# Computing the u and p projections of a hybrid decoder step with features on the partitions

## The chip, the cores and the metric

The kernel runs on one core of a Trainium2 chip, in float32. The metric is the device time of one execution in microseconds (us). The core's engines are TensorE (PE; its weight loads are the row PEld), VectorE (DVE), ScalarE (ACT), GpSimd (POOL) and SyncE (SP), which issues most DMAs. Every engine works through its own queue in order, and they wait for one another on semaphores.

## The reference

One inference step of one layer, over 1024 prompt tokens and 64 new tokens (8 sequences of 8), width 1024:

```
h = rmsnorm(x, norm1_g);  proj = h @ w_in                       # 1024 -> 3 x 512
uv = gelu(proj[..., :1024]);  u = uv[..., :512]
v = layernorm(uv[..., 512:], a_norm_g, a_norm_b);  p = proj[..., 1024:]
ya = u * (tril(W_s[h]) @ v_chunk + b[h])                        # 4 heads, chunks of 128 positions
yb = ((trailing mean of p over 2/4/8/16) - p) @ b_w[g] * b_scale    # 4 groups of 128 features
x = x + concat(ya, yb) @ w_out
h2 = rmsnorm(x, norm2_g)
x = x + top-1 of 4 groups, then top-2 of 8 SwiGLU experts (h2);  y = rmsnorm(x, normf_g)
# also returned: the last 15 rows of p of the prompt and of each new sequence, and v of the new tokens
```

## The kernel before

**Front.** The tokens are nine tiles: tiles 0 to 7 of 128 prompt tokens, tile 8 ("sample") of 64. `pipeline` (L342) writes every engine's queue as steps: step i has the projections and mixers of tile i (`cur`), the residual, second norm and router of tile i-1 (`prev`), the ranking of tile i-2 (`pprev`) and the first norm and turn of tile i+1 (`nxt`). Steps 2 to 6 are a hardware loop, the others straight code.

In a step TensorE makes for `cur` the products v, u, p (L1182: hT, features on partitions and tokens as columns, is the stationary operand; w_in streams in 512 columns; eight contraction slices of 128). ScalarE takes gelu of v and u and a copy of p. VectorE normalises v (L929 to L944). TensorE forms z = W_s v for the four heads (L1193), with tokens on partitions. It forms the pooled means by products with constant band matrices (L1205), one for the tile itself and one for the tile before, whose p VectorE keeps in `ptail` (L957); these products leave features on the partitions. VectorE gates z with bias and u into `ya` (L953). TensorE turns xn of tile i+1 into the PSUM banks 0 and 1 (`wide`, L1131), turns `ya` (L1131), and multiplies the pooled means by b_w (L1221). VectorE reads the turned xn into hT (L822) and scales yb (L964). TensorE turns xn2 of tile i-1 into the same banks 0 and 1, which is why it waits for hT_ready; then it multiplies by the first half of w_out (L1239), makes the router's logits (L1247) and the second half of w_out (L1255). Tile 8 does its products in two halves of the array (L1144, L1153), 64 tokens each.

**Expert part.** 32 experts in blocks of 96, 80 or 64 rows. For each block w1 and w3 are the stationary operand, 64 features at a time into one half of the array, and the tokens are the columns (L1285, contraction slice outer, group of 128 features inner); the down product is L1306. Each expert's 6 MB of weights come in six chunks into a ring of 18 (three experts). SyncE issues a load when the chunk in its place is used (L472), for the first experts in places of w_in and x that the front has left: L456 after the sample's projections, L475 to L484 after the first rows are gathered and the last out_b. GpSimd writes the token table (L553), gathers and scatters rows. ScalarE reads the table's first column (L733) once the table of tiles 0 to 7 is written; this releases the first gather.

## Time and profile before

| | us |
|---|---|
| median of 3 runs (lowest, highest) | 977.61 (976.02, 978.34) |
| the profiled execution | 981.23 |
| its span | 979.6 |
| TensorE busy in the span | 900.6 |
| VectorE, ScalarE, GpSimd busy | 257.5, 110.0, 155.4 |

Rows of the profile read as: busy time, instructions, mean ns of one, and what ended an idle time ("<-"). A float32 matmul shows as two instructions. Start times are us from the start of the span. PEclk is the granted TensorE clock as a share of full speed. The front ends at about 397 us, the expert part at about 943 us.

### The profile page before, as it was taken

Reading aid. Unit: us, or ns where it says so; the run is one execution under the profiler, and the core shown is the slowest. Engines: PE = TensorE matmul, PEld = TensorE weight load, DVE = VectorE, ACT = ScalarE, POOL = GpSimd, SP = SyncE. Lnnn points to the kernel's source line nnn. Section 1 sums busy time; section 2 is a strip of 40 time slices with the busy share of each in tenths; the row PEclk is TensorE's granted clock in tenths of the full one; section 3 lists DMA queues with packets and bytes.
Section 4 is the critical chain, followed back from the end, with each engine's and each line's share of the span. In section 5 each row is a group of like instructions: output and inputs, shape, how many; then the busy total and the mean of one; then the engine's idle time right before and its main releaser. Section 6 shows DMA issues by size and latency. Waiting matters only on the chain.

```text
span 979.6 us, 24674 instructions
## 1 busy us (share of the span) xinstructions
PE 900.6 (92%) x10538; PEld 596.2 (61%) x10538; DVE 257.5 (26%) x779; ACT 110.0 (11%) x173; POOL 155.4 (16%) x260
## 2 busy tenths in 40 slices
PE   4999999999999995799999999999999999989940
PEld 2545555454554563767868686868686768567630
DVE  1443454625445356150010101010101010100106
ACT  0210111101111011101001000001010101001013
POOL 1000100000000000211213131312122313113110
PEclk9999999999999997699999999999999999979985
DMA  8870200201021027799999999999999999999738
GB/s 340 275 292 1 87 31 12 86 0 43 8 78 44 3 91 286 301 399 392 353 393 404 393 407 391 408 389 409 389 408 391 402 394 401 398 405 400 270 70 321
DMA packets 57440, 258.70 MB, mean 264 GB/s; under 512 B 10809, under 2 KB 11889, under 8 KB 40356
## 3 DMA queue, kind: packets, MB, share of 16 engines
q1 hardware_dynamic: 47484, 238.51, 60.7%
q0 software_dynamic: 9264, 19.36, 8.1%
q8 instruction: 41, 0.67, 0.3%
q10 hardware_dynamic: 640, 0.07, 0.1%
q14 instruction: 11, 0.09, 0.0%
HBM read 240.86 MB, written 25.04 MB: 271 GB/s over the span
## 4 chain that ended last, share of the span: by engine, by line
PE 54%; issue 3%; DVE 2%; DMA 2%; DVEq 0%; ACT 0%; SPq 0%; POOLq 0%; POOL 0%
PE ps L1285 31%; PE ps L1306 19%; PE ps L1131 3%; DVE big L1115 1%; DMA big<-x_rows 1%; DMA x_rows<-xn,sidx 0%; PE ps L1319 0%; DMA xg<-h_rows,oidx 0%; PE ps L1314 0%; DVE ssf L806 0%; DVE ssf L805 0%; DVE ssf L808 0%; DVEq L80 0%; ACT junk L784 0%; DMA slot_table<-ids,dest 0%
## 5 line engine op out<-in xcount | busy, mean ns | idle before, releaser
L1285 PEld LDWEIGHTS ps<-hT,big 128*64 128x64 f32 x8192 | 299.5, 139 | 41.1 <-issue 39.1
L1285 PE MATMUL ps<-hT,big 128*64 128x80 f32 (+2 forms) x8192 | 308.6, 236 | 13.0 <-issue 10.7
L1306 PE MATMUL ps<-big,poolT 128*80 128x512 f32 (+2 forms) x512 | 191.2, 594 | 0.6 <-issue 0.6
L1182 PE MATMUL ps<-big,hT 128*128 128x512 f32 x384 | 168.9, 599 | 4.3 <-DMA big<-in_w_in 2.9
L1182 PEld LDWEIGHTS ps<-big,hT 128*128 128x128 f32 x384 | 72.8, 192 | 95.0 <-issue 88.0
L1306 PEld LDWEIGHTS ps<-big,poolT 128*80 128x80 f32 (+2 forms) x512 | 64.5, 149 | 103.1 <-issue 102.0
L1079 DVE TENSOR_TENSOR poolT<-u,ps 128x320 f32<-128x320 f32 (+2 forms) x32 | 15.5, 486 | 421.7 <-PE ps L1285 421.7
L577 POOL DMA_INDIRECT x_rows<-xn,sidx x22 | 32.9, 1495 | 274.1 <-ACT xn L763 253.1
L553 POOL DMA_INDIRECT slot_table<-ids,dest x18 | 18.9, 1052 | 305.4 <-DVE dest L879 263.3
L1239 PE MATMUL ps<-big 128*128 128x512 f32 x128 | 56.4, 593 | 0.9 <-DVE big L964 0.9
L1255 PE MATMUL ps<-big 128*128 128x512 f32 x128 | 57.0, 598 | 0.0
L763 ACT ACTIVATE xn<-ps,gslot 80x1024 f32<-80x1024 f32 (+1 forms) x21 | 23.3, 1110 | 259.1 <-PE ps L1306 259.1
L1239 PEld LDWEIGHTS ps<-big 128*128 128x128 f32 x128 | 23.7, 190 | 28.0 <-issue 27.8
L1255 PEld LDWEIGHTS ps<-big 128*128 128x128 f32 x128 | 23.7, 190 | 27.6 <-issue 27.3
L572 POOL DMA_INDIRECT gslot<-gate_rows,pidx x32 | 32.2, 1007 | 21.3 <-POOL sidx L623 14.0
L996 DVE TENSOR_TENSOR hT<-ps,g2t 128x768 f32<-128x768 f32 (+1 forms) x32 | 28.0, 875 | 27.6 <-PE ps L1131 18.3
L1131 PE MATMUL ps<-ident,xn 128*128 128x128 f32 (+1 forms) x144 | 21.3, 297 | 13.2 <-DVE xn L817 8.4
L577 POOL DMA_INDIRECT x_rows<-bands,sidx x10 | 14.6, 1460 | 89.2 <-DVE bands L1086 76.0
L754 ACT ACTIVATE u<-ps 128x320 f32<-128x320 f32 (+2 forms) x32 | 13.9, 435 | 125.2 <-PE ps L1285 125.2
L1131 PEld LDWEIGHTS ps<-ident,xn 128*128 128x128 f32 (+1 forms) x144 | 18.6, 196 | 14.5 <-issue 9.6
L953 DVE SCALAR_TENSOR_TENSOR big<-ps,bst,u 128x128 f32<-128x128 f32 x32 | 9.0, 345 | 67.6 <-PE ps L1193 67.6
L695 ACT ACTIVATE xn<-big 128x1024 f32 (+2 forms) x9 | 9.5, 1057 | 150.3 <-DVE big L911 150.3
(184 smaller groups left out, 561.2 us busy)
## 6 DMA issues: line engine op xcount, KB each, us to landing
big<-in_exp_w SPq DMA_DIRECT2D x192, 1024.0 KB
big<-in_w_in SPq DMA_DIRECT2D x4, 1536.0 KB, 13.4
big<-in_w_out SPq DMA_DIRECT2D x2, 2048.0 KB, 14.4
x_rows<-big SPq DMA_DIRECT2D x8, 512.0 KB
h_rows<-xn SPq DMA_DIRECT2D x8, 512.0 KB, 2.9
big<-x_rows SPq DMA_DIRECT2D x8, 512.0 KB, 7.2
out_y_prompt<-big SPq DMA_DIRECT2D x8, 512.0 KB, 2.8
big<-in_x_prompt SPq DMA_DIRECT2D x1, 3072.0 KB, 11.3
```

The costliest lines, as they stand in the source:

```text
L553: pool.indirect_dma_start(slot_table, bass.IndirectOffsetOnAxis(ap=dest[0:m, j, c:c + 1], axis=0), ids[0:m, j, c, :], None, bounds_check=N ...
L572: pool.indirect_dma_start(dst, None, gate_rows, bass.IndirectOffsetOnAxis(ap=idx.bitcast(U32), axis=0), bounds_check=last_pair, oob_is_err ...
L577: pool.indirect_dma_start(x3_rows, bass.IndirectOffsetOnAxis(ap=idx.bitcast(U32), axis=0), src, None, bounds_check=last_row, oob_is_err=Tr ...
L763: act.activation(ys[s][0:m, :], ps[0:m, 5:7, :].rearrange("p a n -> p (a n)"), ACT.Copy, scale=gslot[s][0:m, 0:1]).then_inc(y_ready, 1)
L996: dve.tensor_tensor(xT[:, :, 0:ways * i].rearrange("p k (w i) -> p k w i", i=i), wide.rearrange("p k (i w) -> p k w i", w=WAYS)[:, :, 0:wa ...
L1079: dve.tensor_tensor(hhT[:, :, 0:m], s1T[:, :, 0:m], up3[:, :, 0:m], ALU.mult).then_inc(hhT_ready, 1)
L1131: last = pe.transpose(ps[:, bank + c // 4, (c % 4) * P:(c % 4) * P + m], xs[:, c, :], ident[0:m, 0:m])
L1182: last = pe.matmul(ps[0:m, bank, :], hT[:, k, 0:m], win[:, k, part * AW:(part + 1) * AW], start=(k == 0), stop=(k == KD - 1))
L1239: last = pe.matmul(ps[0:m, 6, :], yT[:, k, 0:m], wout[:, k, 0:512], start=(k == 0), stop=(k == KD - 1))
L1255: last = pe.matmul(ps[0:m, 7, :], yT[:, k, 0:m], wout[:, k, 512:D], start=(k == 0), stop=(k == KD - 1))
L1285: last = pe.matmul(out[c * w:(c + 1) * w, j, 0:m], up_weights(n)[:, k, j * P + c * w:j * P + (c + 1) * w], xT[:, 4 * half + k, 0:m], start ...
L1306: last = pe.matmul(ps[first:first + m, 5 + cols, :], hhT[:, 2 * half + k, 0:m], down_weights(n)[:, k, cols * 512:(cols + 1) * 512], start= ...
```

## The change

In tiles 0 to 7 u and p are computed with features on the partitions and tokens as columns: w_in is the stationary operand, 64 features at a time into alternate halves of the array, and hT streams in 128 columns. The contraction slices are the outer and the groups of 128 features the inner loop. v stays as it was; the order is v, p, u. z is computed turned as well, by exchanging the operands. So `ya` and the pooled means are born in the form that the output product needs: the turns of `ya` and the band products are gone. The trailing sums are made by VectorE along the columns (`pool_tile`), with 16 columns carried over from the tile before (`pT[:, :, 0:HALO]`), and the bias, now along the columns, comes from a tile broadcast to all partitions. ScalarE copies p into pT and no longer copies the pooled means and the turned ya. The bias and the share numbers live in `gf`, so the final gain is loaded into it late, in tile 8. The last rows of p of the prompt are turned back by four small products in tile 7 and stored from `xg[1]`. Tile 8 is computed as before.

```diff
-        vg, p, ya, ptail = [big[:, third + (NT + 1) * D + i * AW:third + (NT + 1) * D + (i + 1) * AW] for i in range(4)]
+        vg, ya, p, _ = [big[:, third + (NT + 1) * D + i * AW:third + (NT + 1) * D + (i + 1) * AW] for i in range(4)]
...
-        band = bands[:, 0:AW].rearrange("p (g n) -> p g n", n=P)
-        band_prev = bands[:, AW:D].rearrange("p (g n) -> p g n", n=P)
+        pT = bands[:, 0:GROUPS * (HALO + P)].rearrange("p (g n) -> p g n", n=HALO + P)
+        sum4 = bands[:, GROUPS * (HALO + P):GROUPS * (HALO + P) + 3 * (HALO + P)].rearrange("p (g n) -> p g n", n=HALO + P)
+        tail = third + (NT + 1) * D + 2 * AW
+        sum2 = big[:, tail:tail + GROUPS * (HALO + P)].rearrange("p (g n) -> p g n", n=HALO + P)
...
+        bias = gf[:, 0:AW].rearrange("p (h n) -> p h n", n=P)
+        share = gf[:, AW:AW + GROUPS * HALO].rearrange("p (g n) -> p g n", n=HALO)
...
-            load(bst[:, :], bs_th)
-            load(band_first[:, :, :], c_band_first)
+            load(bias_in[:, :], bs_th.rearrange("t h -> (t h)").partition_broadcast(P))
...
-            load_late(gf[:, :], normf_g.partition_broadcast(P))
...
             sp.wait_ge(v_ready, NT)
+            sp.wait_ge(yaT_ready, LAST)
+            sp.dma_start(gf[:, :], normf_g.partition_broadcast(P)).then_inc(in_gf, 16)
             sp.dma_start(v_s[0].rearrange("b s c -> (b s) c"), v[0:NS, :]).then_inc(outs, 16)
             sp.wait_ge(proj_p, NT)
+            sp.wait_ge(proj_u, NT)
             for n in range(CH):
                 sp.dma_start(chunk_dst(n, n), chunk_src(FIRST, n)).then_inc(chunk_in[n], 16)
...
+            pool.wait_ge(outs, 16 * OUTS)
...
-                    act.wait_ge(proj_u, i + 1)
-                    reached(act, ya_ready, i)
-                    take(u, 3, cur, ACT.Gelu).then_inc(u_gelu, 1)
-                    act.wait_ge(proj_p, i + 1)
-                    reached(act, ptail_ready, i)
+                    if cur != "sample":
+                        act.wait_ge(proj_p, i + 1)
+                        reached(act, halo_ready, i + 1)
+                        act.activation(pT[:, :, HALO:], ps[:, 4, :].rearrange("p (g n) -> p g n", n=P), ACT.Copy)\
+                            .then_inc(p_copied, 1)
+                        act.wait_ge(proj_u, i + 1)
+                        reached(act, yaT_ready, i)
+                        take(u, 3, cur, ACT.Gelu).then_inc(u_gelu, 1)
+                    if isinstance(i, int) and i == LAST - 1:
+                        act.wait_ge(trash_zeroed, 16)
+                        act.wait_ge(rows_turned, 1)
+                        act.activation(xg[1][0:HALO, 0:AW], ps[0:HALO, 4, :], ACT.Copy).then_inc(rows_copied, 1)
                     if cur == "sample":
...
                 reached(dve, proj_p, i)
+                reached(dve, proj_u, i)
...
+            def pool_tile(i, first):
+
+                at = lambda t, lo, by=0, gs=slice(0, GROUPS): t[:, gs, lo - by:HALO + P - by]
+                dve.wait_ge(p_copied, i + 1)
+                reached(dve, yb_done, i)
+                dve.tensor_tensor(at(sum2, 2), at(pT, 2), at(pT, 2, 1), ALU.add).then_inc(sum_step, 1)
+                dve.wait_ge(sum_step, 4 * i + 1)
+                dve.tensor_tensor(at(sum4, 4, 0, slice(0, 3)), at(sum2, 4, 0, slice(1, 4)), at(sum2, 4, 2, slice(1, 4)), ALU.add)\
+                    .then_inc(sum_step, 1)
+                dve.wait_ge(sum_step, 4 * i + 2)
+                dve.tensor_tensor(at(sum2, 8, 0, slice(2, 4)), at(sum4, 8, 0, slice(1, 3)), at(sum4, 8, 4, slice(1, 3)), ALU.add)\
+                    .then_inc(sum_step, 1)
+                dve.wait_ge(sum_step, 4 * i + 3)
+                dve.tensor_tensor(sum4[:, 2, HALO:], sum2[:, 3, HALO:], sum2[:, 3, HALO - 8:HALO - 8 + P], ALU.add)\
+                    .then_inc(sum_step, 1)
+                dve.wait_ge(sum_step, 4 * i + 4)
+                sums = (sum2[:, 0, :], sum4[:, 0, :], sum2[:, 2, :], sum4[:, 2, :])
+                for g, w in enumerate(WINDOWS):
+                    last = dve.scalar_tensor_tensor(poolT[:, g, :], sums[g][:, HALO:], 1.0 / w, pT[:, g, HALO:],
+                                                    ALU.mult, ALU.subtract)
+                if first:
+                    last.then_inc(share_step, 1)
+                    dve.wait_ge(share_step, 8)
+                    for g in range(GROUPS):
+                        last = dve.tensor_tensor(poolT[:, g, 0:HALO], sums[g][:, HALO:2 * HALO], share[:, g, :], ALU.mult)
+                    last.then_inc(share_step, 1)
+                    dve.wait_ge(share_step, 9)
+                    last = dve.tensor_tensor(poolT[:, :, 0:HALO], poolT[:, :, 0:HALO], pT[:, :, HALO:2 * HALO], ALU.subtract)
+                last.then_inc(poolT_ready, 1)
+                dve.tensor_copy(pT[:, :, 0:HALO], pT[:, :, P:HALO + P]).then_inc(halo_ready, 1)
+
...
+                if isinstance(i, int) and i == 0:
+                    dve.wait_ge(in_small, 16 * len(small))
+                    dve.tensor_copy(bias[:, :, :], bias_in.rearrange("p (t h) -> p h t", h=HEADS)).then_inc(share_step, 1)
+                    dve.wait_ge(share_step, 7)
+                if cur and cur != "sample":
+                    pool_tile(i, cur == "first")
+                    dve.wait_ge(z_done, i + 1)
+                    dve.tensor_tensor(ya[:, :], ps[:, 5, :], bias.rearrange("p h n -> p (h n)"), ALU.add).then_inc(z_biased, 1)
+                    dve.wait_ge(z_biased, i + 1)
+                    dve.wait_ge(u_gelu, i + 1)
+                    reached(dve, out_b, i)
+                    dve.tensor_tensor(yT[:, 0:HEADS, :], ya.rearrange("p (h n) -> p h n", n=P),
+                                      u.rearrange("p (h n) -> p h n", n=P), ALU.mult).then_inc(yaT_ready, 1)
+                if cur == "sample":
...
-                    for bank, part, free, done in () if cur == "sample" else \
-                            ((2, 1, v_gelu, proj_v), (3, 0, u_gelu, proj_u), (4, 2, p_copied, proj_p)):
-                        reached(pe, free, i)
-                        if bank == 2:
-                            reached(pe, logits_ready, i - 1)
+                    else:
+                        reached(pe, v_gelu, i)
+                        reached(pe, logits_ready, i - 1)
                         for k in range(KD):
-                            if isinstance(i, int) and i == 0 and bank == 2 and k % 2 == 0:
+                            if isinstance(i, int) and i == 0 and k % 2 == 0:
                                 pe.wait_ge(in_win[k // 2], 16)
-                            last = pe.matmul(ps[0:m, bank, :], hT[:, k, 0:m], win[:, k, part * AW:(part + 1) * AW],
+                            last = pe.matmul(ps[:, 2, :], hT[:, k, :], win[:, k, AW:2 * AW],
                                              start=(k == 0), stop=(k == KD - 1))
-                        last.then_inc(done, 1)
+                        last.then_inc(proj_v, 1)
+                        for bank, part, free, done in ((4, 2, p_copied, proj_p), (3, 0, u_gelu, proj_u)):
+                            reached(pe, free, i)
+                            for k in range(KD):
+                                for j in range(AW // P):
+                                    for c in range(SPLIT):
+                                        at = part * AW + j * P + c * NS
+                                        last = pe.matmul(ps[c * NS:(c + 1) * NS, bank, j * P:(j + 1) * P],
+                                                         win[:, k, at:at + NS], hT[:, k, :], start=(k + j == 0),
+                                                         stop=(k == KD - 1), skip_group_check=True)
+                            last.then_inc(done, 1)
...
-                        last = pe.matmul(ps[0:m, 5, h * P:(h + 1) * P], w[0:m, h, 0:m],
-                                         v[0:m, h * P:(h + 1) * P], start=True, stop=True)
+                        if cur == "sample":
+                            last = pe.matmul(ps[0:m, 5, h * P:(h + 1) * P], w[0:m, h, 0:m],
+                                             v[0:m, h * P:(h + 1) * P], start=True, stop=True)
+                        else:
+                            last = pe.matmul(ps[:, 5, h * P:(h + 1) * P], v[:, h * P:(h + 1) * P], w[:, h, :],
+                                             start=True, stop=True)
                     last.then_inc(z_done, 1)
...
-                    parts = {"first": [(p, band_first, P)], "mid": [(p, band, P), (ptail, band_prev, P)],
-                             "sample": [(p, band_s, NS), (state, band_state, DEC * STATE)]}[cur]
-                    w = P // SPLIT if cur == "sample" else P
...
+                    if isinstance(i, int) and i == LAST - 1:
+                        pe.wait_ge(p_copied, i + 1)
+                        for g in range(GROUPS):
+                            last = pe.matmul(ps[0:HALO, 4, g * P:(g + 1) * P], pT[:, g, P:HALO + P], ident[:, :],
+                                             start=True, stop=True, skip_group_check=True)
+                        last.then_inc(rows_turned, 1)
...
-                    pe.wait_ge(ya_ready, i + 1)
-                    turn(ya, m, yaT_done, HEADS, 5)
+                    if cur == "sample":
+                        pe.wait_ge(ya_ready, 1)
+                        turn(ya, m, yaT_done, HEADS, 5, whole=True)
                     pe.wait_ge(poolT_ready, i + 1)
+                    reached(pe, x2a_ready, i)
```

TensorE in a middle step of the loop, from the projections to the first half of the output product. Names: ps is PSUM, big holds w_in, w_out, p, ya and yT, done_early the masked W_s and b_w, bands the band matrices. Before:

```order
L1182 MATMUL ps<-big,hT 128x512 [waits p_copied]
L1182 MATMUL ps<-big,hT 128x512 x7
L1193 MATMUL ps<-v,done_early 128x128 [waits rank_taken,v_ready]
L1193 MATMUL ps<-v,done_early 128x128 x3
L1205 MATMUL ps<-bands,big 128x128 [waits x2a_ready,ptail_ready,p_copied]
L1205 MATMUL ps<-bands,big 128x128 x7
...
L1131 MATMUL ps<-ident,xn 128x128 [waits h2T_ready,xn_ready]
L1131 MATMUL ps<-ident,xn 128x128 x7
L1131 MATMUL ps<-ident,big 128x128 [waits ya_ready]
L1131 MATMUL ps<-ident,big 128x128 x3
L1221 MATMUL ps<-poolT,done_early 128x128 [waits poolT_ready]
L1221 MATMUL ps<-poolT,done_early 128x128 x3
```

And in the change, to the turns of xn2 and the output product (L1326):

```order
L1258 MATMUL ps<-hT,big 64x128 [waits u_gelu]
L1258 MATMUL ps<-hT,big 64x128 x63
L1274 MATMUL ps<-done_early,v 128x128 [waits rank_taken,v_ready]
L1274 MATMUL ps<-done_early,v 128x128 x3
...
L1199 MATMUL ps<-ident,xn 128x128 [waits h2T_ready,xn_ready]
L1199 MATMUL ps<-ident,xn 128x128 x7
L1308 MATMUL ps<-poolT,done_early 128x128 [waits x2a_ready,poolT_ready]
L1308 MATMUL ps<-poolT,done_early 128x128 x3
L1199 MATMUL ps<-ident,xn 128x128 [waits hT_ready,x2n_ready]
L1199 MATMUL ps<-ident,xn 128x128 x7
L1326 MATMUL ps<-big 128x512 [waits ybT_ready,yaT_ready]
L1326 MATMUL ps<-big 128x512 x7
```

Each projection is 64 matmuls of 64x128 in place of eight of 128x512. The band products (L1205) and the turns of ya (L1131 from big) are gone; everything else keeps its place.

VectorE in the same step, from the last operation on v to the scaling of yb. Before:

```order
L944 TENSOR_TENSOR v<-v,done_early 128x512 [waits ln_step]
L953 SCALAR_TENSOR_TENSOR big<-ps,bst,u 128x128 [waits yaT_done,u_gelu,z_done]
L953 SCALAR_TENSOR_TENSOR big<-ps,bst,u 128x128 x3
L957 COPY big<-big 128x512 [waits pooled]
L822 TENSOR_TENSOR hT<-ps,g1t 128x1024 [waits proj_p,xT_done]
L964 TENSOR_TENSOR big<-ps,bsc 128x512 [waits out_b,yb_done]
```

In the change, where bands holds pT and sum4, big also sum2, and gf the bias:

```order
L906 TENSOR_TENSOR big<-bands 128x4x142 [waits yb_done,p_copied]
L908 TENSOR_TENSOR bands<-big 128x3x140 [waits sum_step]
L911 TENSOR_TENSOR big<-bands 128x2x136 [waits sum_step]
L914 TENSOR_TENSOR bands<-big 128x128 [waits sum_step]
L919 SCALAR_TENSOR_TENSOR poolT<-big,bands 128x128 [waits sum_step]
...
L930 COPY bands<-bands 128x4x16
L1010 TENSOR_TENSOR big<-ps,gf 128x512 [waits z_done]
L1014 TENSOR_TENSOR big<-big,u 128x512 [waits out_b,u_gelu,z_biased]
L842 TENSOR_TENSOR hT<-ps,g1t 128x1024 [waits proj_u,proj_p,xT_done]
L1031 TENSOR_TENSOR big<-ps,bsc 128x512 [waits out_b,yb_done]
```

The pooling stands between v and z in VectorE's queue, and two operations of 512 columns stand before hT where four of 128 and a copy stood. At the start of tile 0 a rearranging copy of the bias and the share operations come on top.

## Rows read from the trace of the kernel before

**Rows 1.** The page: the chain that ended last, by engine.
```profile
PE 54%; issue 3%; DVE 2%; DMA 2%; DVEq 0%; ACT 0%; SPq 0%; POOLq 0%; POOL 0%
```

**Rows 2.** Stretches: busy us (count) of PE, PEld, DVE, ACT, POOL; PEclk, DMA share, GB/s.
```profile
353.00:395.00 42.00, 29.23 (x256) 18.75 (x252) 24.75 (x101) 8.73 (x16) 5.45 (x6) 0.79 0.60 220
...
600.00:650.00 50.00, 49.61 (x873) 37.28 (x868) 4.76 (x7) 4.21 (x6) 12.91 (x19) 1.00 1.03 400
```

**Rows 3.** Timeline, TensorE, a middle tile: start us, us, what, [idle before].
```profile
161.54 1.05 PE L1193 MATMUL ps<-v,done_early 128*128 128x128 f32 x8
...
162.43 2.01 PE L1205 MATMUL ps<-bands,big 128*128 128x128 f32 x16
...
164.27 1.05 PE L1131 MATMUL ps<-ident,xn 128*128 128x128 f32 x8
...
165.16 0.65 PE L1131 MATMUL ps<-ident,big 128*128 128x128 f32 x4
...
165.64 1.06 PE L1221 MATMUL ps<-poolT,done_early 128*128 128x128 f32 x8
...
166.73 1.13 PE L1131 MATMUL ps<-ident,xn 128*128 128x128 f32 x8
...
167.70 7.03 PE L1239 MATMUL ps<-big 128*128 128x512 f32 x16
...
183.05 12.26 PE L1182 MATMUL ps<-big,hT 128*128 128x512 f32 x28
```

**Rows 4.** Timeline, VectorE, the same tile and the next one's v.
```profile
162.63 1.13 DVE L953 SCALAR_TENSOR_TENSOR big<-ps,bst,u 128x128 f32<-128x128 f32 x4 [9.26 <-PE ps L1193]
...
165.36 1.22 DVE L822 TENSOR_TENSOR hT<-ps,g1t 128x1024 f32<-128x1024 f32 x1 [0.46 <-PE ps L1131]
...
166.74 0.69 DVE L964 TENSOR_TENSOR big<-ps,bsc 128x512 f32<-128x512 f32 x1 [0.15 <-PE ps L1221]
...
194.88 0.69 DVE L944 TENSOR_TENSOR v<-v,done_early 128x512 f32<-128x512 f32 x1
```

**Rows 5.** Timeline, TensorE, tile 7.
```profile
330.34 1.05 PE L1193 MATMUL ps<-v,done_early 128*128 128x128 f32 x8
...
336.71 7.10 PE L1239 MATMUL ps<-big 128*128 128x512 f32 x16
```

**Rows 6.** Chain of waits, expert part (96, then 80 rows): start us, us, what.
```profile
512.70 10.56 PE ps L1285 x256
523.26 1.09 PE ps L1131 x8
...
531.22 9.32 PE ps L1285 x255
...
541.64 6.87 PE ps L1306 x16
```

**Rows 7.** Timeline, TensorE, the sample's projections.
```profile
352.23 10.58 PE L1144 MATMUL ps<-big,hT 128*64 128x256 f32 x96
```

**Rows 8.** Timeline, tile 0: the end of v, and the output product.
```profile
35.01 0.69 DVE L944 TENSOR_TENSOR v<-v,done_early 128x512 f32<-128x512 f32 x1
...
42.72 7.10 PE L1239 MATMUL ps<-big 128*128 128x512 f32 x16 [0.88 <-DVE big L964]
```

**Rows 9.** End of the front: stretches as in rows 2; timelines of GpSimd and ScalarE.
```profile
385.00:387.00 2.00, 1.63 (x16) 1.49 (x14) 0.30 (x2) 0.00 (x0) 0.00 (x0) 0.50 0.65 243
387.00:389.00 2.00, 0.00 (x0) 0.00 (x0) 1.69 (x10) 0.00 (x0) 0.00 (x0) 0.50 0.08 29
...
382.42 1.16 POOL L553 DMA_INDIRECT slot_table<-ids,dest  x1 [0.30 <-issue]
...
388.97 2.49 ACTq L733 DMA_DIRECT2D oidx<-slot_table  x4
```

**Rows 10.** The sample's turns of xn2 (timeline), and the clock then (stretch).
```profile
367.17 1.97 PE L1131 MATMUL ps<-ident,xn 128*128 128x128 f32 x8
...
367.00:368.00 1.00, 1.00 (x10) 0.88 (x7) 0.42 (x1) 0.00 (x0) 0.00 (x0) 0.50 0.23 43
```

More of the change, by code:

```diff
@@ L1201, in step @@
-                    w = P // SPLIT if cur == "sample" else P
-                    for g in range(GROUPS):
-                        for n, (src, bnd, kk) in enumerate(parts):
-                            for c in range(P // w):
-                                last = pe.matmul(ps[c * w:(c + 1) * w, 6, g * P:g * P + m],
-                                                 src[0:kk, g * P + c * w:g * P + (c + 1) * w], bnd[0:kk, g, 0:m],
-                                                 start=(n == 0), stop=(n == len(parts) - 1), skip_group_check=True)
```

145 lines of the change are left out of this document (81 added, 64 removed).

## The prediction

> **What bounds the kernel now.** I read the chain of waits first: more than half of the span is TensorE work with nothing late in front of it [rows 1]. Then the table of stretches. In the expert part TensorE is busy 49.61 of 50 us while the DMA engines are full (share 1.03). Between the two parts (353 to 395 us) TensorE is busy 29.23 of 42 us at a mean clock of 0.79 [rows 2]. Only tiles of the front are changed, so the next view is the timeline of one middle tile [rows 3]. There TensorE has no idle time: four z products, eight band products, eight turns of xn, four of ya, four products by b_w, eight turns of xn2, then the output product. From the first z product (161.54) to the first output product (167.70) is 6.16 us. The gate, copy and scaling of VectorE beside it are in [rows 4]: z is taken 1.09 us after its first product started, and xn2 is turned 0.15 us after hT ends (165.36 + 1.22 = 166.58, then 166.73), because hT must have been read out of the two banks into which xn2 is turned.
>
> Does time saved in the front reach the end? The sync queue loads most of the first two experts behind the last tile's products, and from there the loads of the expert part wait for the first gathered rows or for a buffer in use. Both are anchored to the front's end, so I pass a shift on in full.
>
> **Part by part, tiles 1 to 7.** *Gone from TensorE:* the eight band products (162.43 to 164.27, 1.84 us) and the four ya turns (165.16 to 165.64, 0.48 us), together 2.3 us a tile [rows 3]. *What is late next:* VectorE. It used to gate z in 1.13 us; now it adds the bias (PSUM, 512 columns) and multiplies by u (512 columns). Both are priced at the 0.69 us of a 512 column operation [rows 4]. From the first z product: 1.09, bias to 1.78, product to about 2.45, hT (1.22) to 3.65, release 0.15, so xn2 turns at 3.80, plus 0.97 (166.73 to 167.70) gives 4.77. The scaling after hT (0.69) ends by 4.4 and is hidden. TensorE's own work would take only 0.89 + 0.89 + 1.09 + 0.97 = 3.84, so it now idles some 0.9 us before xn2. Saving 6.16 - 4.77 = 1.39 us; six tiles give 8.3. Tile 7 takes 336.71 - 330.34 = 6.37 us before [rows 5]; in the change its hT for the 64 samples waits for turns that stand behind four new products (rows turned back for the pool state, some 0.95 us), and my chain gives 4.75, a saving of 1.6.
>
> *The u and p products.* Before, each is 16 instructions of 512 columns, 0.429 us each (6.87 us for 16) [rows 3, 6]. Now each is 128 instructions of 64 weights by 128 columns, alternating between the halves of the array. The nearest rows are the expert products, of the same form and loop order: 256 instructions of 96 columns in 10.56 us, 41.3 ns each; 80 columns take 9.32 us [rows 6]. At 0.429/1024 us a column in one half, 32 more columns cost 13.4 ns, so 54.7 ns each and 13.99 us for both products, against 13.74: +0.25. Behind such halves, eight turns take 1.09 us and not the 0.89 of a tile's xn turns [rows 3, 6]: +0.20. Sum +0.45 a tile, seven tiles 3.15. Bounds: nothing below (halves side by side do the same columns); above, the sample's halves of 256 columns took 10.58/96 = 110.2 ns where 107.3 is even, 2.9 ns too many [rows 7], which by 256 is 0.75, with 0.20 it is 0.95 a tile, 6.65 in all. I take 3.15, because the 96 column row is nearest in width and form.
> By the Trainium skill (TensorEngine Tiling (Array Packing), Key Properties) every change of tiling mode drains the engine, so entering the halves after v would cost as much as leaving them. The expert rows do not show that: the 16 down instructions in front of halves take 6.87 us, exactly 16 x 0.429 [rows 6]. By the rule 0.2 us more would come in each tile, and the sum below would be -3.4 instead of -4.8.
>
> *The pooling on VectorE.* New before the bias add: sums of 568, 420, 272 and 128 columns, four operations of 128, a copy of 64. At 0.69 for 512, thus about 0.16 + columns/960, the sums are 0.75, 0.59, 0.44, 0.29; the four 128s cost 1.13 as the four of the gate did; with gaps 3.4 us. p is ready 13.9 + 0.8 us after v's products start, and v itself at 195.57 - 183.05 = 12.5 [rows 3, 4]. So the chain ends near 18.1, while z cannot be taken before 22. The u product hides it with 3.9 us to spare; if the cover went, the excess would count in full. The copy of p and gelu of u on ScalarE, and the later release of hT by u instead of p, lie in the same order as before and cost nothing. The two dropped ScalarE copies were hidden.
>
> **Tile 0.** Here the cover is thin. v is ready only at 35.70 [rows 8], since ScalarE's queue has the second x tile, which lands late, in front of the gelu. Bias rearranged (0.5), pooling (3.4), the first tile's share operations (0.8) end at 40.3; bias add and product to 41.7, hT to 42.9, scaling to 43.5, output product near 43.65 instead of 42.72 [rows 8]. This chain does not run through the products, so it contains their cost: +0.95 (0 if the operations overlap better, +2.5 if the clock falls in the gap). The share numbers and the iota fall into the wait for w_in: nothing. Fewer early loads: nothing, w_in stands ahead of them.
>
> **Between the parts.** The final gain vector (0.5 MB broadcast) is now loaded in front of the six expert chunks. The DMA engines are full until about 386.3 (share 0.65 in 385 to 387), and the token table written at 382.42 is seen by ScalarE only at 388.97 [rows 9], with little DMA work after 387. I read that as: the table waits for the chunks, and the first gather for the table. 0.52 MB at the chunks' rate (six of 1.05 MB and the small rest in 17.3 us, 0.42 MB/us) is 1.25 us, less what goes into the empty start: I take +1.0, bounds 0 and 1.5.
>
> **Sum.** -8.3 - 1.6 + 3.15 + 0.95 + 1.0 = -4.8 us. The profiled execution took 981.23 us (span 979.6), which becomes 976.4. The median of the runs is 3.6 lower, 977.61, so I forecast 977.61 - 4.8 = 972.8. Best end of all terms: -9.9 + 0 + 0 + 0 = -9.9, 967.7. Worst: -9.9 + 6.65 + 2.5 + 1.5 = +0.8, 978.4. About 0.2% (2 us) is what can be told from no change.
>
> **Rivals.**
> - *The halves cost what the sample's do.* For it: rows 7, and more instructions to fetch in straight code. Against: the 96 column expert row. Products 6.65 instead of 3.15: -1.3 us, 976.3, no change.
> - *Slower: the clock falls in every middle tile.* After the sample's small products the turns of xn2 ran at 0.50, 1.97 us instead of 0.97 [rows 10, 3]. The new tile has fewer band products and about 0.9 us of idle between its turns. Price a fall at 1.0 for the turns and 0.6 for the start of the output product: 1.6 x 7 = 11.2, thus +6.4 us, 984.0. It decides from a fall in three tiles of seven (4.8 us). Against it: tile 0 had 0.88 us idle at the same place [rows 8] and its output product still took 0.43 an instruction.
>  The Trainium skill (TensorE: Matmul & The Clock Gate, Part 4: PE-mode transpose) says that transposes do not count as busy for the clock. It speaks for this rival: two of the four pieces left are turns. The trace agrees in so far as nothing here contradicts it; that 1.4 us of turns stood together before without a fall does not decide it.
> - *The gain is given back behind the front.* Were the table or the expert loads late by themselves (the DMA engines are full in the expert part [rows 2]), some 3 to 5 us would vanish: 976 to 978, no change. Against it: every load there waits for something of the front.
> - *VectorE's pooling overruns its cover.* It takes 3.9 us more than I work out, in each tile; beyond that every us costs 7. At 5 us of excess: -4.8 + 7.7 = +2.9, 980.5.
>
> **Chances.** Forecast 0.64; halves dearer 0.13; clock 0.10; given back 0.08; pooling overruns 0.05. The forecast's case leaves faster with about 0.62, and the two no-change cases add 0.03. No change: 0.19, slower: 0.16 (clock, pooling, and a part of the given-back case). The likeliest case alone spans 968 to 977. For eight in ten I take 967.5 to 980.5, which takes in the bounds of the sum and the pooling case and leaves out the clock.
>
> **What would show it.** Right: a middle tile shorter by about 0.95 us; 4.8 us from z to the output product, with an idle of TensorE before the xn2 turns ended by hT; 54 to 55 ns per half instruction; the pooling done before z; tile 0's output product about 1 us later than before; table seen about 1 us later after its writing. Wrong: half instructions above 57 ns, a granted clock under 1.00 inside tiles 1 to 7, z waiting for the pooling operations, or the expert part longer than before by more than 2 us.

## The result, and the profile after

The changed kernel took 985.25 us (median of 10 runs, 980.72 to 990.75) against 977.48 us (10 runs, 976.02 to 979.70) of the kernel before on the same chip: ratio 1.0076, 95% interval 1.0055 to 1.0097. It is 7.8 us slower; the forecast was 4.8 us faster. Its profiled execution took 985.02 us (span 983.3), that of before 981.23 (span 979.6), which lies above before's median. So the two traces differ by 3.7 us only, and sizes are taken from stretches that stand in both. A ratio of two kernels leaves out runs that lie more than 1.5% above the fastest of their kernel; here there are none.

**The middle tiles came out much as forecast.** A middle tile on TensorE, to be laid beside [rows 3] (start us, us, what, idle before):

```profile
150.69 14.19 PE L1258 MATMUL ps<-hT,big 128*64 128x128 f32 x256
164.81 1.16 PE L1274 MATMUL ps<-done_early,v 128*128 128x128 f32 x8
165.81 1.04 PE L1199 MATMUL ps<-ident,xn 128*128 128x128 f32 x8
166.69 1.06 PE L1308 MATMUL ps<-poolT,done_early 128*128 128x128 f32 x8
168.70 1.13 PE L1199 MATMUL ps<-ident,xn 128*128 128x128 f32 x8 [0.96 <-DVE hT L842]
169.67 7.03 PE L1326 MATMUL ps<-big 128*128 128x512 f32 x16
```

From z to the output product it is 169.67 - 164.81 = 4.86 us (forecast 4.77, before 6.16), with 0.96 us of idle that ends with hT (forecast some 0.9). The u and p products take 164.81 - 150.69 = 14.12 us (forecast 13.99). VectorE in the same tile, beside [rows 4]:

```profile
158.57 0.75 DVE L906 TENSOR_TENSOR big<-bands 128x568 f32<-128x568 f32 x1 [2.41 <-ACT bands L718]
...
161.60 0.19 DVE L930 COPY bands<-bands 128x64 f32<-128x64 f32 x1
166.01 0.69 DVE L1010 TENSOR_TENSOR big<-ps,gf 128x512 f32<-128x512 f32 x1 [4.22 <-PE ps L1274]
```

The pooling takes 3.2 us and leaves 4.22 us of idle before z: it is hidden. Tile 7, beside [rows 5], takes 5.12 us (before 6.37, forecast 4.75). TensorE has no idle in it: what it does there is 5.12 us of work.

```profile
330.36 1.16 PE L1274 MATMUL ps<-done_early,v 128*128 128x128 f32 x8
...
335.48 7.11 PE L1326 MATMUL ps<-big 128*128 128x512 f32 x16
```

**Tile 0 is dearer.** The end of v on VectorE, and TensorE, beside [rows 8]:

```profile
36.27 0.69 DVE L1002 TENSOR_TENSOR v<-v,done_early 128x512 f32<-128x512 f32 x1
...
41.44 1.16 PE L1308 MATMUL ps<-poolT,done_early 128*128 128x128 f32 x8 [2.00 <-DVE poolT L928]
44.69 9.55 PE L1326 MATMUL ps<-big 128*128 128x512 f32 x16 [2.10 <-DVE big L1031]
54.08 7.03 PE L1342 MATMUL ps<-big 128*128 128x512 f32 x16
```

and the second half of the output product before:

```profile
49.66 7.03 PE L1255 MATMUL ps<-big 128*128 128x512 f32 x16
```

The output product starts 1.97 us later than before (forecast 0.95), and takes 9.55 us instead of 7.10: TensorE has idled 2.00 and then 2.10 us, with eight products between, and the granted clock is 0.50 from 44.7 to 49.6 us. The second half starts at 54.08 against 49.66 before: +4.4 us. The lower clock costs a different amount in each execution: with the same order of work the first half takes 7.11 us in the trace of a_pad220 below, 8.51 to 8.80 in three others and 10.01 in that of a_pad64.

**Between the parts time is gained, and not by the change alone.** GpSimd, ScalarE's queue and TensorE, beside [rows 9, 10]:

```profile
365.73 1.16 PE L1199 MATMUL ps<-ident,xn 128*128 128x128 f32 x8
...
379.63 1.16 POOL L561 DMA_INDIRECT slot_table<-ids,dest  x1 [0.30 <-issue]
385.31 2.49 ACTq L752 DMA_DIRECT2D oidx<-slot_table  x4
...
393.67 1.97 PE L1401 MATMUL ps<-ident,xg 128*128 128x128 f32 x8 [4.25 <-DMA xg<-h_rows,oidx]
```

The table is seen 5.7 us after its writing (before 6.55), and the first gathered rows are turned at 393.67 instead of 397.38: the front is 3.7 us shorter in these two traces. Only 1.44 us of that stand at the sample's turns of xn2 (365.73 against 367.17 [rows 10]). The next 1.36 us are the clock: in the trace of before it is at its lower level there [rows 10], in that of after it is not (the eight turns take 1.16 us instead of 1.97). The last 0.9 us is the table. The front of b_both below is word for word that of before, and in its trace the clock does not fall there and the rows are turned at 394.99. So the same front varies by 2.4 us from one trace to another, and 3.7 us is more than the change is shown to give.

**The loss is in the expert part.** One pass of an expert loop is three blocks, 840 matrix instructions (a stretch counts 842, since it cuts one at either end) and as many weight loads. The first loop has six passes, the second three. The five passes of the first loop after its first one, kernel after (stretches as in [rows 2]):

```profile
506.70:555.80 49.10, 48.82 (x842) 36.50 (x844) 4.77 (x8) 4.21 (x6) 12.12 (x18) 1.00 1.02 399
555.80:613.60 57.80, 50.94 (x842) 37.82 (x844) 4.77 (x8) 4.21 (x6) 12.10 (x18) 0.97 1.01 384
613.60:662.70 49.10, 48.82 (x842) 36.51 (x844) 4.78 (x8) 4.21 (x6) 12.09 (x18) 1.00 1.02 399
662.70:720.60 57.90, 50.96 (x842) 38.03 (x843) 4.74 (x7) 4.21 (x6) 12.11 (x18) 0.97 1.00 376
720.60:769.60 49.00, 48.72 (x842) 36.45 (x844) 4.82 (x8) 4.21 (x6) 12.10 (x18) 1.00 1.02 398
```

The same view of before: a pass of the first loop (all five are like it), and the last two of the second; then the timeline of the very last, with its idle time:

```profile
558.40:607.60 49.20, 48.81 (x842) 36.52 (x844) 4.79 (x8) 4.21 (x6) 12.10 (x18) 1.00 1.02 399
...
803.90:851.60 47.70, 47.38 (x842) 34.90 (x844) 4.74 (x8) 4.16 (x6) 12.09 (x18) 1.00 1.02 400
851.60:909.10 57.50, 51.16 (x842) 38.06 (x842) 4.67 (x8) 4.16 (x6) 12.08 (x18) 0.91 1.02 400
...
857.83 2.11 PE L1285 MATMUL ps<-hT,big 128*64 128x80 f32 x33 [2.73 <-issue]
862.93 10.65 PE L1285 MATMUL ps<-hT,big 128*64 128x80 f32 x223 [2.98 <-issue]
```

Two passes in the one kernel, one in the other, take 58 us instead of 48 or 49. The work in them is the same. The timeline of after where such a pass begins, and its last idle time:

```profile
555.69 3.65 PE L1393 MATMUL ps<-big,poolT 128*64 128x512 f32 x16
562.21 3.55 PE L1372 MATMUL ps<-hT,big 128*64 128x96 f32 x47 [2.87 <-issue]
567.60 5.50 PE L1372 MATMUL ps<-hT,big 128*64 128x96 f32 x128 [1.84 <-issue]
573.53 3.54 PE L1372 MATMUL ps<-hT,big 128*64 128x96 f32 x81 [0.43 <-issue]
...
612.13 0.34 PE L1372 MATMUL ps<-hT,big 128*64 128x64 f32 x4 [1.42 <-issue]
```

TensorE idles for "issue": the profile shows no engine and no load that is late. The DMA queues tell what it waits for. Kernel after, the stretches 510 to 555 us (a good pass; no row for the instruction queue) and 556 to 612 us (queue, kind: packets, MB, share):

```profile
q1 hardware_dynamic: 3001, 16.32, 88.3%
...
q1 hardware_dynamic: 3463, 19.60, 87.3%
...
q8 instruction: 9, 0.15, 1.0%
```

Nine packets of 16 KB: the loop's instructions are fetched anew. On the page q8 has 56 packets after and 41 before:

```profile
q8 instruction: 56, 0.92, 0.4%
```

Between 510 and 760 us after has 18 of them (two passes), before none; before has 9 in its last pass of the second loop. Counted in the traces from branch to branch, a pass executes 1,693 TensorE instructions (its waits and the jump are among them), and before's first two groups of three blocks, where all code is new, needed 13 packets: a packet is about 256 instructions, a pass 6.6 packets. Counted in the same way, with the loop of the front taken once, the change makes TensorE's program ahead of the first loop 1,666 instructions longer, six packets and 130 instructions.

Code that comes for the first time costs little. In before there is no "issue" idle in the first pass of either loop. In after there are 1.86 us in that of the first loop, of which this is the larger part, and 1.59 us in that of the second:

```profile
505.27 0.34 PE L1372 MATMUL ps<-hT,big 128*64 128x64 f32 x4 [1.37 <-issue]
```

What costs much is a jump back to code that is gone.

The Trainium skill (Runtime: NRT & Kernel Launch, Instruction fetch mechanics) says that TensorE's instruction memory holds 2,048 instructions, is filled in blocks of 256, and that a taken branch to a block that is not there stalls. The packets agree with the block; the size no run here tests. As an estimate from that size, a pass of 6.6 blocks would fit if it touches seven of the eight blocks and one more is fetched ahead, and not if it touches eight. The same section also speaks of only two lines and of purely sequential fetching; here the measurement differs and decides: in before five passes of this loop ran without a packet.

### The profile page after: what moved, and what is told of

It reads as the page before. It is cut to its first block and busy times, and to the rows that moved or that the text cites. A ratio compares the mean times of both kernels' runs of the same rounds, so it can differ in the third digit from the quotient of the medians.

```text
span 983.3 us, 28026 instructions
## 1 busy us (share of the span) xinstructions
PE 890.1 (91%) x12186; PEld 640.9 (65%) x12186; DVE 280.7 (29%) x838; ACT 100.9 (10%) x158; POOL 155.3 (16%) x262
## 5 line engine op out<-in xcount | busy, mean ns | idle before, releaser
L1372 PEld LDWEIGHTS ps<-hT,big 128*64 128x64 f32 x8192 | 298.8, 139 | 50.0 <-issue 47.8
L1258 PEld LDWEIGHTS ps<-hT,big 128*64 128x64 f32 x2048 | 111.6, 137 | 6.1 <-issue 6.1
L1258 PE MATMUL ps<-hT,big 128*64 128x128 f32 x2048 | 113.6, 273 | 0.0
L1249 PE MATMUL ps<-big,hT 128*128 128x512 f32 x128 | 59.3, 615 | 3.6 <-DMA big<-in_w_in 2.2
L1326 PE MATMUL ps<-big 128*128 128x512 f32 x128 | 58.8, 614 | 2.1 <-DVE big L1031 2.1
L1342 PE MATMUL ps<-big 128*128 128x512 f32 x128 | 57.0, 598 | 0.0
L1249 PEld LDWEIGHTS ps<-big,hT 128*128 128x128 f32 x128 | 24.4, 197 | 33.1 <-issue 26.9
L1326 PEld LDWEIGHTS ps<-big 128*128 128x128 f32 x128 | 24.6, 198 | 30.7 <-issue 30.5
L1342 PEld LDWEIGHTS ps<-big 128*128 128x128 f32 x128 | 23.7, 190 | 27.6 <-issue 27.3
L1199 PE MATMUL ps<-ident,xn 128*128 128x128 f32 (+1 forms) x144 | 20.5, 289 | 18.6 <-DVE xn L836 8.2
```

The lines of the kernel that those rows point to most:

```text
L1199: last = pe.transpose(ps[:, bank + c // 4, (c % 4) * P:(c % 4) * P + m], xs[:, c, :], ident[0:m, 0:m])
L1249: last = pe.matmul(ps[:, 2, :], hT[:, k, :], win[:, k, AW:2 * AW], start=(k == 0), stop=(k == KD - 1))
L1258: last = pe.matmul(ps[c * NS:(c + 1) * NS, bank, j * P:(j + 1) * P], win[:, k, at:at + NS], hT[:, k, :], start=(k + j == 0), stop=(k == KD ...
L1326: last = pe.matmul(ps[0:m, 6, :], yT[:, k, 0:m], wout[:, k, 0:512], start=(k == 0), stop=(k == KD - 1))
L1342: last = pe.matmul(ps[0:m, 7, :], yT[:, k, 0:m], wout[:, k, 512:D], start=(k == 0), stop=(k == KD - 1))
L1372: last = pe.matmul(out[c * w:(c + 1) * w, j, 0:m], up_weights(n)[:, k, j * P + c * w:j * P + (c + 1) * w], xT[:, 4 * half + k, 0:m], start ...
```

## The experiments

Theory I: the place of the two expert loops in the instruction blocks decides which passes are fetched again. Theory II: the fetches are a by-product, and the expert part is longer because the weight stream starts at another time. All ratios are to runs of before made beside them on the same chip; its median was 969.45 us on the chip of the first four kernels (where a good pass takes 47.7 us) and 977.95 and 977.78 us on those of the others (49.0). The kernel after was not run again beside them, so what is said against it goes by the two ratios to before.

**Half a block of padding behind the front.** Each float32 product is four TensorE instructions (two matrix instructions, two weight loads). The edit, in the kernel after; in b_pad128 the same in the kernel before, and in a_pad64 half as much in after:

```
+            def pad(n):
+                for _ in range(n // 4):
+                    pe.matmul(ps[0:32, 0, 0:8], ident[0:32, 0:32], ident[0:32, 0:8], start=True, stop=True)
+
+            pad(128)
             pe.wait_ge(rows_in[0], 16)
```

> The kernel after, with 32 matmuls of 32x8 (128 TensorE instructions, each fp32 matmul being four) put where TensorE waits for the first gathered rows. Nothing else changes; the front, the data and the DMAs are those of after. Theory I (instruction fetches): the expert part is 8 us longer than before because the first expert loop now stands across one 16 KB block of instructions more than before, so its third and fifth pass are fetched again (18 instruction packets between 550 and 720 us, none there before). Half a block of padding puts it back: those 18 packets go, the second loop is fetched again in its last pass as in before (9 packets), expert part 546 us instead of 554, total 977 us (975 to 979). Theory II (the weight stream starts at another point of time against the end of the front, and the fetches are only a by-product): no change, 985 us (983 to 987).

> The kernel before, with the same 128 TensorE instructions of padding at the same place. Theory I: its first expert loop gets the position in the instruction blocks that after has; instruction packets between 550 and 720 us appear, those of the second loop's last pass go; expert part 554 us instead of 546, total 985 us (983 to 988). Theory II: front and weight stream are those of before, so 977.5 us (976 to 979).

> The kernel after with 64 TensorE instructions of padding at the same place (a quarter of a block). Theory I: by my reckoning of the positions both loops stand badly: refetches in passes three and five of the first loop and in the last of the second, 27 packets, expert part 554 + 5 = 559 us, total 990 us (984 to 992). Theory II: 985 us as without padding.

Measured: a_pad128 981.55 us, ratio 1.0113 (1.0093 to 1.0133); b_pad128 975.22, 1.0062 (1.0046 to 1.0077); a_pad64 1020.27, 1.0505 (1.0468 to 1.0543). In a_pad128 the two long passes of the first loop are gone, as theory I says, but the second loop now has two long ones where I expected one:

```profile
506.80:554.50 47.70, 47.70 (x842) 35.80 (x842) 4.72 (x7) 4.21 (x6) 12.12 (x18) 1.00 1.02 399
794.40:853.80 59.40, 50.40 (x842) 37.60 (x840) 4.74 (x8) 4.16 (x6) 12.08 (x18) 0.91 1.02 400
853.80:912.30 58.50, 49.83 (x842) 37.12 (x840) 4.64 (x8) 4.16 (x6) 12.08 (x18) 0.91 1.02 400
```

So the total was a miss and the first loop a hit. In b_pad128 the pattern of after appears in the kernel before, with 18 packets between 510 and 760 us:

```profile
507.40:555.10 47.70, 47.70 (x842) 35.80 (x842) 4.73 (x7) 4.22 (x6) 12.12 (x18) 1.00 1.02 399
555.10:612.50 57.40, 50.14 (x842) 37.73 (x844) 4.76 (x7) 4.22 (x6) 12.11 (x18) 0.97 1.02 395
```

Front and loads are those of before there, so theory II, which expects no change, is refuted. (Its one long pass of the second loop is gone, too.) In a_pad64 every one of the five passes is long; the idle time at the start of the first of them:

```profile
513.52 0.87 PE L1372 MATMUL ps<-hT,big 128*64 128x96 f32 x15 [2.72 <-issue]
518.92 11.51 PE L1372 MATMUL ps<-hT,big 128*64 128x96 f32 x241 [4.52 <-issue]
```

with 38 packets between 510 and 760 us; the second loop has no long pass. Sixty-four instructions made the kernel after 4.3% slower by the ratios, 5% slower than before. I had expected three long passes in all, not five in the one loop.

**Tile 0's order.** The kernel after; in step 0 ScalarE's square of the next x stands behind the gelu of v, and VectorE's norm of it behind the v chain. VectorE's part of the edit:

```
-                if nxt:
+                start = isinstance(i, int) and i == 0
+                if nxt and not start:
                     norm1(i + 1, m_of(nxt), xres[0:m_of(nxt), i + 1, :])
...
                     dve.tensor_tensor(v[0:m, :], v[0:m, :], ab[0:m, :], ALU.add).then_inc(v_ready, 1)
+                if start:
+                    norm1(i + 1, m_of(nxt), xres[0:m_of(nxt), i + 1, :])
```

> The kernel after; in tile 0 alone ScalarE squares the next tile's x (which lands at 28.6 us) after the gelu of v instead of before it, and VectorE makes that tile's norm after the v chain instead of ahead of it. TensorE's program is word for word that of after. Output product of tile 0 should start at 41.7 us instead of 44.7, with its clock at full (first half 7.0 us instead of 9.55): front 3 to 5.5 us shorter. Theory I: the refetches stay (18 packets), expert part 554 us, total 980 to 982 us. Theory II: the expert part starts 3 to 5 us earlier and so meets another phase of the weight stream; its length changes by some us from 554.

Measured: 969.84 us, ratio 1.0005 (0.9995 to 1.0015), so 0.7% under after by the ratios. I had expected 980 to 982 us against 977.5, a ratio of 1.003 to 1.005; where the other 2 to 4 us went was not followed. The output product starts 3.6 us earlier than in after and at full clock:

```profile
41.09 7.10 PE L1334 MATMUL ps<-big 128*128 128x512 f32 x16 [1.55 <-DVE big L1039]
48.03 7.03 PE L1350 MATMUL ps<-big 128*128 128x512 f32 x16
```

and the second half 6.05 us earlier, a little more than the expected 3 to 5.5. TensorE's program is unchanged, the expert part starts 4.5 us earlier (first gathered rows at 389.21), and the long passes stay where they were (57.7 and 57.6 us, 18 packets): once more against theory II.

**Both loops well placed.** a_both has the 128 instructions ahead of the first gathered rows and 104 more between the loops, which a branch skips; b_both is the kernel before with the second piece alone:

```
+                if between and lo == CLASSES[1][0]:
+                    between()
                 with eng.Fori(lo, hi) as h:
...
-            triples(pe, block_triple)
+            def skipped():
+                with pe.If(pe.snap(pe.to_reg(0)) > 0):
+                    pad(104)
+
+            triples(pe, block_triple, skipped)
```

> The kernel after with both expert loops moved to a good place: 128 instructions of padding ahead of the first gathered rows, and between the two loops 108 instructions that a branch jumps over. By the first runs a pass of a loop that is fetched again takes 57 to 60 us instead of 46 to 48; after has two such passes. Theory I: none left, expert part 20 us shorter than in after, total 12 us under before (ratio 0.987 to 0.989; 957 us if before is 969). If only the sum of fetched bytes counted and not the place, nothing would change against after (ratio 1.0076).

> The kernel before with its second loop moved by the same 108 skipped instructions (its first loop stands well already). Theory I: its one fetched pass goes, 6 to 10 us less than before (ratio 0.990 to 0.994). The pair a_both against b_both is then the change itself without fetches: the traces' fronts say a_both is shorter by 3.7 us, my prediction said 4.8. If the gain of the front is given back in the expert part by something other than the fetches, the pair comes out equal.

> The kernel after with 220 instructions of padding ahead of the first gathered rows and none between the loops. In parts of a block and counted from where after's first loop starts, clean places seen so far for a loop of this length are 0.49 to 0.86, bad ones 0 to 0.25. The first loop comes to 0.86, the second (6.61 blocks further) to 0.47, just outside what has been seen. If both are clean: as a_both, ratio 0.988. If the second is fetched in one or both of its last passes: 10 to 24 us more, ratio 0.998 to 1.012.

Measured: a_both 965.27 us, ratio 0.9864 (0.9843 to 0.9884); b_both 967.40, 0.9890 (0.9872 to 0.9907); a_pad220 977.75, 0.9954 (0.9929 to 0.9980). a_both has no long pass and one packet between 510 and 760 us:

```profile
q8 instruction: 1, 0.02, 0.0%
...
554.60:603.70 49.10, 48.83 (x842) 36.53 (x844) 4.81 (x8) 4.21 (x6) 12.10 (x18) 1.00 1.02 399
...
847.80:895.10 47.30, 47.13 (x842) 34.68 (x844) 4.69 (x8) 4.16 (x6) 12.08 (x18) 1.00 1.02 400
```

Against after by the ratios that is 2.1%, some 20.7 us, for two fetched passes; between the two traces the expert part, from the first gathered rows to the last down product, is 18.6 us shorter. b_both gains 10.6 us on before for one fetched pass. Both gains are a little larger than expected. The pair a_both and b_both, the change itself without fetches, differs by 2.1 us, less than the 3.7 or 4.8 I had named; the intervals of the two ratios overlap, so this pair alone does not show a gain. The front shows 1.6 us of it:

```profile
393.41 1.97 PE L1408 MATMUL ps<-ident,xg 128*128 128x128 f32 x8 [0.99 <-DMA xg<-h_rows,oidx]
```

in a_both, and in b_both

```profile
394.99 1.97 PE L1320 MATMUL ps<-ident,xg 128*128 128x128 f32 x8 [5.14 <-DMA xg<-h_rows,oidx]
```

From there to the end of the last pass of the second loop it is 501.7 and 501.0 us: without fetches the expert part keeps its length within 0.7 us.

a_pad220 is a miss. Its profiled run has long passes of 57.7 and 57.1 us in the first loop, at a place that I had held for clean, and its runs spread from 967.73 to 985.45 us where those of a_both stay within 5 us. The ratio is over eight of its twelve runs; the median of all twelve is that of before. Its padding is not free either: the rows are turned 10.1 us after the table is seen, 8.4 in after. The second loop, of whose place I was unsure, has none. And a_pad64's second loop, of the same length and by my count at the same place in a block as the first loop here, was clean too: the place alone does not settle it. Near a border between places a pass is fetched in some executions and not in others; that its fastest runs have no fetched pass fits their time, but only the profiled one has a trace.

The traces so far together, with the place counted in parts of a block of 256 instructions from where after's first loop starts, and the number of long passes behind the loop's first one:

| kernel | first loop: place, long of 5 | second loop: place, long of 2 |
|---|---|---|
| a_both, b_both | 0.50, 0 | 0.5, 0 |
| a_pad128 | 0.50, 0 | 0.12, 2 |
| before | 0.49, 0 | 0.11, 1 |
| after, a_tile0 | 0, 2 | 0.62, 0 |
| b_pad128 | 0.99, 2 | 0.61, 0 |
| a_pad64 | 0.25, 5 | 0.87, 0 |
| a_pad220 | 0.86, 2 | 0.48, 0 |

Loops at places from 0.48 to 0.62 were clean, those from 0.99 over 0 to 0.25 were not, and at 0.86 or 0.87 one was clean and one was not. The kernels after and b_pad128 differ by 1,538 instructions ahead of the first loop, two more than six blocks, and have the same pattern, which is for the block of 256; a padding by one whole block, which should change nothing, was not run.

**Less weight traffic.** The kernel after, with only a quarter of each chunk loaded from the fourth block on; it leaves out the other three quarters of those weights, so it shows times alone:

```
-                    load_chunk(turn[s], n)
+                    if c < 4:
+                        sp.dma_start(chunk[n][:, 0:CHW // 4], chunk_src(turn[s], c)[:, 0:CHW // 4]).then_inc(chunk_in[n], 16)
...
```

> The kernel after, but from the fourth expert block on only a quarter of each weight chunk is loaded (the rest of a buffer keeps older weights; left out is three quarters of the weight traffic). TensorE's program is that of after, so its loop stands as badly as there. Theory Ia (a fetched pass is long because its first packets come behind the weights in the shared DMA engines): the 18 refetched packets stay, but the two stalls of 2.9 and 1.8 us at the start of such a pass shrink to under 1 us in sum and the pass is at most 3 us longer than its neighbours, against 8.7 in after. Theory Ib (a fetch has its own latency of some 2.5 us, whatever else is moved): the stalls and most of the 8.7 us stay.

Measured: 966.82 us (2 runs), ratio 0.9888 (0.9861 to 0.9916). The 18 packets did not stay: there are 11 between 510 and 760 us, and only one pass, the first loop's last, is fetched, and it is 4.0 us longer than its neighbours, not 8.7:

```profile
601.60:650.70 49.10, 48.81 (x842) 36.55 (x844) 4.81 (x8) 4.22 (x6) 12.13 (x18) 1.00 0.48 133
699.70:752.80 53.10, 50.56 (x842) 37.95 (x842) 4.73 (x8) 4.22 (x6) 12.13 (x18) 0.97 0.47 125
...
705.45 12.43 PE L1376 MATMUL ps<-hT,big 128*64 128x96 f32 x256 [2.24 <-issue]
```

Neither form of the theory was right. The first stall after the jump is hardly shorter with less traffic (2.24 us at a DMA share of 0.5, 2.87 at 1.0), as Ib says; the later ones (1.84, 0.43 and, near the pass's end, 1.42 us) are gone but for 0.16, as Ia says. That is one pass; at other places the first stall was 3.9 to 4.6 us with the full traffic (a_pad128, a_pad220). The rest is the clock, which fell for a part of it: the 256 products take 12.43 us instead of 10.73. And which pass is fetched depends on the timing of the transfers as well as on the place; how, these runs don't tell.

**The change alone, with tile 0 mended.** b_best is b_both with the order of a_tile0, a_best is a_both with it.

> a_both with tile 0's order as in a_tile0 (square and norm of tile 1 behind the v chain). The two gains touch different stretches, so they add: a_tile0 stood some 7 us under after, a_both should stand 20 under it; 27 us under after, ratio to before 0.980 (0.978 to 0.983).

> b_both (the kernel before without refetches) with the order of tile 0 that a_best has: square and norm of tile 1 behind the v chain. In the kernel before the v chain ends 1.9 us before TensorE's z in tile 0, so the order frees nothing there: same time as b_both, ratio to before 0.989 (0.987 to 0.991).

> a_best once more, beside b_best on one chip: what the turned front is worth with neither refetches nor the late tile 0. Seven tiles at 0.8 us and more, the sample tile's share less tile 0's: my prediction's sum was 4.8 us; so ratio 0.984 against 0.989 of b_best, some 5 us less. If the front's gain is lost behind it all the same, the two come out within 2 us.

Measured: a_best 962.04 us, ratio 0.9838 (0.9823 to 0.9853), some 23 us under after where I had expected 27: the two gains do not add in full. In the later comparison it took 962.25, 0.9845 (0.9827 to 0.9863); b_best 967.84, 0.9896 (0.9879 to 0.9913), the same as b_both, as expected. The new front with neither handicap is 5.6 us faster than the old one, 5.0 by the ratios, and here the intervals lie apart. a_best beats both kernels: 1.6% under before, 2.3% under after.

## Why the prediction was wrong, point by point

- **The step that failed:** "Both are anchored to the front's end, so I pass a shift on in full", taken as: the expert part keeps its length. The anchoring is right (501.7 against 501.0 us in the clean pair). But I held code that isn't edited for code that takes the same time. Its place in TensorE's instruction blocks moved by 130 instructions beyond whole blocks. That cost two fetched passes in the first loop, 16.8 us over its five passes in the traces, and saved one in the second, 9.7 us over its three; 1.3 us more went ahead of them, up to the end of the first loop's first pass, and 0.3 came back at the end. That is the +8.1 us of the expert part. By the clean kernels the two effects are 20.7 and 10.6 us. The spans of the two traces differ by -3.7 in the front, +8.1, and -0.7 behind the last down product: +3.7. The medians differ by 7.8; before's profiled run lies 3.7 above its median, and its front alone is 2.4 later than that of b_both, which accounts for most of the rest.
- The rows were there to see: before itself had a pass of 57.5 us among passes of 47.7, and 41 packets of instructions on its page. I never looked at what ended the idle time in the part that the change doesn't touch, and named instruction fetches only as a price of straight code, where they cost little. The section of the Trainium skill cited above has the branch rule; it belonged among the rivals.
- **The front as a whole:** too large. Up to the sample's turns of xn2 the terms gave -8.3 - 1.6 + 3.15 + 0.95 = -5.8 us, the traces have -1.4; 3.5 of the missing 4.4 us are tile 0's. The clean pair's front has -1.6.
- **Middle tiles:** right. 4.86 us from z to output (4.77), products 14.12 us (14.19 with the dearer turns), a tile's period 41.4 us against 42.2: -0.8 (forecast -0.94).
- **Tile 7:** -1.25 us, forecast -1.6. The chain through VectorE that I priced at 4.75 does not end last there: TensorE's own five pieces do, 5.12 us without a gap.
- **Tile 0:** mis-sized, +4.4 us where I had +0.95 with a bound of 2.5. The chain behind v was priced rightly (36.96 instead of 35.70 for v gives 44.9 by my sum, 44.69 was measured). But v is ready 1.26 us later (36.27 + 0.69 = 36.96 against 35.70), because ScalarE gets the second x tile at 28.65 and not at 27.32 us: in the six traces with the new front and the old order at 28.3 to 29.0, in the three with both old at 27.3 to 27.7 (with the new order it is 27.3 to 28.3, off the path of v). I had put the changed loads at nothing; why the tile lands later stays open. The other 2.45 us are the clock, which I had only as a bound. a_tile0, a_best and b_best show that the order was the cause: by the ratios it frees 2.5 to 7 us with the new front (a_both to a_best, after to a_tile0) and nothing with the old, and in none of their traces is the granted clock below its full level in tile 0.
- **The gain vector's load:** forecast +1.0, nothing of it seen: the table is seen 0.9 us sooner after its writing.
- **Rival of the dearer halves:** out, 55.2 ns an instruction (14.12/256). **Clock in every middle tile:** out, it stayed at full level there; it fell in tile 0 only. **Pooling overruns:** out, 3.2 us. **Given back behind the front:** the loss does stand behind the front, but its mechanism (the table or the loads late) is not what happened, and its 976 to 978 us is far below 985.25.
- The last sentence named the sign that came: "the expert part longer than before by more than 2 us". From the first gathered rows to the last down product it was 8.1 us longer (553.9 against 545.9), yet no case with a chance had a loss of that size there, and the range ended 4.8 us below the time.

## What to carry to other kernels

When an edit changes the number of an engine's instructions, the loops behind it move in the instruction memory. Before a time is forecast, count each long loop's body in blocks of 256, look in the profile for "issue" idle at the start of some passes and for instruction packets in the middle of a loop, and put both outcomes of the move among the cases. A long TensorE loop, such as this of 6.6 blocks, is best measured with a few paddings, or made shorter (not tried here); otherwise 64 instructions can decide more than the edit itself. And work that waits for a late load should stand behind what doesn't need it.

## What the runs showed of the hardware

- The loop of 1,693 TensorE instructions has three conditions by its place: no pass fetched, every second one (57.8 us among 49.1), or all (58.7 to 61.7 us in a_pad64). Why it is every second one stays open. Over five passes the second cost 17 us (262.8 against 246.0) and the third 62 us (301.2 against 239).
- A fetched pass costs more than its stalls, 8.7 us for some 6.6 us of idle, since the clock falls to its lower level after them; in before's long pass the mean clock is 0.91.
- With a quarter of the weights loaded, good passes take the same 49.1 us (DMA share 0.48 instead of 1.02): at this stage TensorE, and not the stream of weights, sets the pace of the expert part.
- Thirty-two products of 32 weights by 8 columns in TensorE's wait for the first rows cost nothing that shows: in a_both they end 0.99 us before the rows come. The 55 of a_pad220 fill the wait and cost some 1.7 us.
